# In the second block's plain attention stages, transposes are issued ahead of the next unit's scores

## What is computed

```python
def hybrid_layer(x, mem, norm_g, w_in, w_out, mem_norm_g, w_mem_kv, qk_g):
    h = rms_norm(x, norm_g)
    proj = jnp.einsum('btd,de->bte', h, w_in)
    ...
    qa = rope(rms_norm(to_heads(a_q, N_HEADS_MOBA), qk_g[0]))
    ka = rope(rms_norm(to_heads(a_k, N_HEADS_MOBA), qk_g[1]))
    oa = from_heads(moba_attention(qa, ka, to_heads(a_v, N_HEADS_MOBA)))
    ...
    ob = from_heads(dilated_attention(qb, kb, to_heads(b_v, N_HEADS_DIL)))
    ...
    om = from_heads(memory_attention(qm, km, to_heads(m_v, N_HEADS_MEM)))
    y = jnp.concatenate([oa * jax.nn.silu(a_g), ob * jax.nn.silu(b_g), om * jax.nn.silu(m_g)], axis=-1)
    return x + jnp.einsum('btd,de->bte', y, w_out)
```

## Time and profile before

| | |
|---|---|
| median of three runs | 2457.07 us (2455.22 to 2459.62) |
| the profiled execution | 2454.57 us, its span 2452.7 us |
| TensorE busy | 2417.9 us, 99% of the span |
| VectorE busy | 1192.6 us, 49% |
| ScalarE busy | 985.3 us, 40% |
| GpSimd busy | 1126.6 us, 46% |
| granted TensorE clock, mean | 0.998 of full |

### The profile page before, as it was taken

How to read it: one execution, slowest core, us unless ns; L and a number is a source line. 1 busy time by engine, 2 the same in 40 slices (tenths; PEclk the granted TensorE clock), 3 DMA queues, 4 the chain that set the end, 5 groups by cost and what they waited for, 6 DMA issues and landing times.

```text
span 2452.7 us, 29903 instructions
## 1 busy us (share of the span) xinstructions
PE 2417.9 (99%) x10934; PEld 1917.5 (78%) x10934; DVE 1192.6 (49%) x1821; ACT 985.3 (40%) x1529; POOL 1126.6 (46%) x828
## 2 busy tenths in 40 slices
PE   9999999999999999999999999999999999999998
PEld 7888888668888888888888768888888676776766
DVE  6444106664555105555106664555126766557553
ACT  5333124553222214222124553222216678456773
POOL 5454455335555445455455335555445332452324
PEclk9999999999999999999999999999999999999999
DMA  4222223212222222222223212222333222222222
GB/s 177 103 86 103 103 86 119 86 57 100 101 103 86 103 101 89 103 87 102 103 86 119 86 58 99 100 103 86 103 135 108 69 84 69 73 104 82 87 68 87
DMA packets 37961, 233.18 MB, mean 95 GB/s; under 512 B 5232, under 2 KB 5360, under 8 KB 11376
## 3 DMA queue, kind: packets, MB, share of 16 engines
q1 hardware_dynamic: 36432, 226.51, 26.8%
q10 hardware_dynamic: 1440, 5.45, 0.6%
HBM read 223.55 MB, written 2.10 MB: 92 GB/s over the span
## 4 chain that ended last, share of the span: by engine, by line
issue 56%; POOL 42%; POOLq 1%; DMA 1%; ACT 0%; SPq 0%; ACTq 0%
POOL w_lo L471 42%; POOLq L481 0%; DMA x_sb<-in_x 0%; POOLq L485 0%; DMA raw<-in_stream 0%; ACT h_hi L1064 0%; ACT w_hi L1021 0%; SPq L434 0%; POOLq L231 0%; ACT sq L1060 0%; ACTq L1442 0%; SPq L435 0%; ACTq L1098 0%; ACT w_hi L1077 0%; ACT hraw L1060 0%
## 5 line engine op out<-in xcount | busy, mean ns | idle before, releaser
L471 POOL TENSOR_TENSOR w_lo<-raw,w_hi 128x512 fp32r<-128x512 f32 x824 | 1126.4, 1398 | 1325.5 <-ACT w_hi L1021 1314.9
L493 PE MATMUL ps<-h_hi,w_hi 128*128 128x512 f32 x2304 | 916.5, 398 | 4.8 <-DVE h_lo L1505 3.9
L495 PE MATMUL ps<-h_hi,w_lo 128*128 128x512 f32 x2304 | 898.5, 390 | 0.0
L494 PE MATMUL ps<-h_lo,w_hi 128*128 128x512 f32 x2304 | 897.8, 390 | 0.0
L1021 ACT ACTIVATE w_hi<-raw 128x1024 fp32r<-128x1024 f32 x410 | 411.6, 1052 | 1163.9 <-PE ps L495 1160.6
L493 PEld LDWEIGHTS ps<-h_hi,w_hi 128*128 128x128 f32 x2304 | 433.2, 188 | 102.2 <-issue 7.5
L495 PEld LDWEIGHTS ps<-h_hi,w_lo 128*128 128x128 f32 x2304 | 432.9, 188 | 92.0
L494 PEld LDWEIGHTS ps<-h_lo,w_hi 128*128 128x128 f32 x2304 | 433.3, 188 | 90.8 <-issue 4.1
L493 PE MATMUL ps<-hid_hi,w_hi 128*128 128x512 f32 x704 | 273.9, 389 | 0.0
L494 PE MATMUL ps<-hid_lo,w_hi 128*128 128x512 f32 x704 | 273.9, 389 | 0.0
L495 PE MATMUL ps<-hid_hi,w_lo 128*128 128x512 f32 x704 | 273.9, 389 | 0.0
(11 more groups left out here) (255 smaller groups left out, 2028.6 us busy)
## 6 DMA issues: line engine op xcount, KB each, us to landing
raw<-in_stream SPq DMA_DIRECT2D x205, 1024.0 KB, 4.8
hraw<-xs SPq DMA_DIRECT2D x96, 64.0 KB, 2.0
x_sb<-in_x SPq DMA_DIRECT2D x4, 512.0 KB, 7.5
out_x<-x_sb SPq DMA_DIRECT2D x8, 256.0 KB, 6.5
raw<-in_stream SPq DMA_DIRECT2D x4, 256.0 KB, 6.8
mem_sb<-in_mem ACTq DMA_DIRECT2D x1, 1024.0 KB, 4.9
rec_sb<-in_recip ACTq DMA_DIRECT2D x2, 512.0 KB, 4.7
memn<-in_mem ACTq DMA_DIRECT2D x1, 1024.0 KB, 5.4
```

The costliest lines, as they stand in the source:

```text
L471: gp.tensor_tensor(w_lo[:, s, c], raw[:, s, c], w_hi[:, s, c].bitcast(F32), ALU.subtract).then_inc(lo_split, 1)
L493: pe.matmul(dst, l_hi, r_hi, start=first, stop=False)
L494: pe.matmul(dst, l_hi, r_lo, start=False, stop=False)
L495: return pe.matmul(dst, l_lo, r_hi, start=False, stop=last)
```

## The change

`attention_step` of TensorE is cut into three parts with unchanged bodies: `begin` (scores of unit `s`), `finish` (outputs) and `turn` (transposes of the unit in front). Before, the order is always begin, finish, turn. After, it is turn, begin, finish in every step but step 0 of the plain stages, and the old one everywhere else. The diff, with the bodies left out:

```diff
             def attention_step(here, before, s, produce):
-                unit = lagged(here, before, s, 0)
-                if unit:
...
-                    scores(stage, u).then_inc(t_scores, 1)
-                unit = lagged(here, before, s, LAG_OUT)
...
-                unit = lagged(here, before, s, LAG_TR)
...
+                def begin():
+                    unit = lagged(here, before, s, 0)
...
+                        scores(stage, u).then_inc(t_scores, 1)
+
+                def finish():
+                    unit = lagged(here, before, s, LAG_OUT)
...
+                        outputs(stage, u).then_inc(t_o, 1)
+
+                def turn():
+                    unit = lagged(here, before, s, LAG_TR)
...
+                        mm.then_inc(t_tr, 1)
+
+                if here and not here.memory and not here.fast and s:
+                    turn()
+                    begin()
+                    finish()
+                else:
+                    begin()
+                    finish()
+                    turn()
```

More of the change, by code:

```diff
@@ L843, in attention_step @@
[L843 to L859, removed]
+                def begin():
+                    unit = lagged(here, before, s, 0)
+                    if unit:
+                        stage, u = unit
+                        if s == 0 and not here.memory:
+                            pe.wait_ge(hn_out, GROUPS * here.l + here.gi + 1)
+                        if u and stage.memory:
+                            pe.wait_ge(t_exp, stage.u0 + u)
+                        elif not stage.memory:
+                            pe.wait_ge(t_exp if u == 0 and before.memory else t_max, stage.u0 + u)
+                        scores(stage, u).then_inc(t_scores, 1)
@@ new lines, in finish @@
+                def finish():
+                    unit = lagged(here, before, s, LAG_OUT)
+                    if unit and ends_group(unit[1]):
+                        stage, u = unit
+                        pe.wait_ge(t_thi, stage.u0 + u + 1)
+                        if not stage.memory:
+                            pe.wait_ge(v_thi, 7 * stage.l + stage.gi)
+                        elif u >= TB:
+                            pe.wait_ge(t_y, stage.outs0 + 1)
+                        outputs(stage, u).then_inc(t_o, 1)
@@ new lines, in turn @@
+                def turn():
+                    unit = lagged(here, before, s, LAG_TR)
+                    if unit:
+                        stage, u = unit
+                        pe.wait_ge(t_att, stage.u0 + u + 1)
+                        if not stage.memory:
+                            pe.wait_ge(t_thi, stage.u0 + u)
+                        elif u >= 2:
+                            pe.wait_ge(t_thi, stage.u0 + u - 1)
+                        for h in range(2):
+                            for kb in range(stage.widths[u] // P):
+                                if stage.memory:
+                                    n = 256 * h + P * kb
+                                    dst, src = ps[:, 2 + u % 2, n:n + P], att2[:, h, 256 * (u % 2) + P * kb:256 * (u % 2) + P * kb + P]
+                                else:
+                                    att = weights(u) if stage.fast else att2
+                                    dst, src = ps[:, 2 + h, P * kb:P * kb + P], att[:, h, P * kb:P * kb + P]
+                                mm = pe.transpose(dst, src, const(C_ID))
+                        mm.then_inc(t_tr, 1)
```

## The result

The changed kernel takes 2473.01 us (median of five runs, 2468.30 to 2474.83); the kernel before took 2455.33 in the same comparison (2452.93 to 2459.62). The ratio is 1.007, with a 95% interval of 1.0059 to 1.0081. The forecast was 2470, in a range of 2464 to 2477. The profiled execution of the changed kernel took 2473.01 us with a span of 2471.1, 18.4 more than that of before.

A forecast was written before the change was run, and what follows sets the result against it. TensorE was taken to bound the kernel. 8 x 1.85 = 14.8, + 0.3, - 1.9 gave +13.2 us on the profiled 2454.57, so 2467.8; 2.5 more for the median gave 2470.3, range 2464 to 2477.

The forecast's parts named there:

- What bounds the kernel: Whole kernel: TensorE, busy for 99% of the span, so the change is worth what it does to its idle time.
- Step 2: Plain stages, eight times: two transposes go ahead of the scores and nothing waits; +0.09 us, by the low end -0.08.
- Step 4: Plain stages, eight times: four transposes ahead of the scores, which start 0.52 us later; next piece +0.10 us.
- The change of kind: TensorE going from transposes to scores: 0.20 us from last transpose to first score, 0.02 to 0.03 as low end.
- Step 6: Plain stages, eight times: transposes wait about 1.9 us for ACT's scaling, scores queue behind; next piece +1.76 us.
- A whole stage: Each of the eight plain stages: 0.09 + 1.76 = 1.85 us longer.
- Stage 2: Its step 2, twice: memory stage's outputs are passed too, ACT's scaling ends 0.1 us late; about 0.15 us more each.
- Given back: Fast stage 6, behind stage 5, twice: TensorE's wait of 1.1 us (line 899) shrinks by 0.97; -1.9 us.
- Rival C: Step 4's exponentials follow ACT's copy, so weights come as before; +6.5 us, 2463.5; chance 0.13.
- Rival D: Plain stages: DVE and ACT's chain paces them, TensorE's delay eats its own waits, not slower; 2460.5; chance 0.04.
- The forecast's own case: Whole kernel: waits grow and the clock holds or falls once; between 2466 and 2472.5, likeliest 2470; chance 0.50.
- rival B: Plain stages: two to five of eight new waits bring a clock fall; +3.4 to +8.5 us, 2473.7 to 2478.8; chance 0.30.

The follow-up runs named there:

- The two experiments with one part each: The turned order in step 6 alone, and in steps 2 and 4 alone, each against the kernel before: 2461.79 us and 2460.00 us against 2455.12.
- The stages-2-to-4 experiment: The turned order in stages 2 to 4 of both layers, stage 5 as before, against the kernel before: 2467.53 us against 2455.51, ratio 1.0051.
- the last two kernels above: New and old order, both with ACT's scaling ahead of two head-norm passes and DVE's reciprocal ahead of the head norm: 2454.02 and 2450.24 us against 2454.68.

## Why the forecast came out as it did

**What bounds the kernel.** Right. Only TensorE's idle time and clock explain the difference.

**Step 2.** Forecast +0.09, measured +0.02 at the place and +0.07 with the piece behind it. **Step 4.** Forecast +0.10, measured +0.02 and +0.05. The change of kind from transposes to scores was right, about 0.2 us; the transition into the transposes was priced slightly too high. In step 4 they start 0.11 behind the last value transpose, not 0.14, and follow each other 0.11 apart, not 0.13. This also makes the scores 0.43 late instead of 0.52.

**Step 6.** Forecast +1.76, with step 4's 0.10 in it, and a wait of 1.9 us, 15 in all. Measured +1.63 and +0.02, a wait of 1.87, 15.0 in all. That the wait came out so close is in part luck. The forecast had TensorE free at 1994.23, but by the earlier trace rows the last matmul ends at 1993.74 + 0.39 = 1994.13, so its own terms give 2.00; weights that were late by 0.43 and not 0.52 took most of this back. The two experiments with one part each split it as the forecast had it: 11.8 us of waits from the order in step 6 alone, and from the late scores of step 4 alone twice the wait of before.

**A whole stage.** Forecast 1.85, measured 1.78 to 1.81. **Stage 2.** Forecast 0.15 more, measured 0.14 more.

**Given back.** Forecast -1.9, measured -2.0, at the place named. The wait for `sq_lo` fell from 1.1 to 0.4 rather than 0.1. DVE's row that waits for the DMA stands there at

```profile
2079.85 0.69 DVE L1905 TENSOR_TENSOR xs<-xs,rope_sb 128x512 f32<-128x512 f32 x1 [2.21 <-DMA hraw<-xs]
```

with 2.21 us of idle time instead of 2.70. The stages-2-to-4 experiment shows that nothing is given back unless the delay comes directly ahead of stage 6.

**Rival C.** Wrong, as it was held to be unlikely. The exponentials are 0.79 us idle behind the copy, and steps 2 and 4 alone made the kernel slower. **Rival D** likewise: no waits but those of stage 6 were eaten.

**The clock, the term that was too small.** The forecast's own case, 2470, had the clock holding or falling once. In the profile it fell three times in plain stages, which is rival B (two to five), though at 1.55 us each and not 1.7; where the 0.15 stay wasn't traced. Without those falls the profiled execution would be at 2473.0 - 4.7 = 2468.3, and without the 1.1 us of the first block at 2467.2; the sum had given 2467.8. So the mechanism and its terms were right within 1 us, and it is the clock that carries the profiled execution above them.

That the median of 2473.0 lies only 3 above the forecast of 2470 is in part luck too. As a difference, the change cost 17.7 us where the sum had 13.2, 4.5 less. The forecast then added 2.5, the distance of the median of three runs from the profiled one; in the comparison with the changed kernel the kernel before has 2455.33, only 0.8 above that execution. This offset hid a part of the missing clock term. The result lies between the forecast's own case (2466 to 2472.5) and B (2473.7 to 2478.8). The step that failed is the reading of a wait of 1.8 us in front of line 493 "followed by no fall" as a sign that 1.9 us would be harmless: it put the clock at nothing, and three falls cost 4.7 us. One execution could not show this. The same wait, in the first block, whose program is the same in both kernels, stands in TensorE's timeline of before and of after as

```profile
535.23 0.50 PE L493 MATMUL ps<-h_hi,w_hi 128*128 128x512 f32 x1 [1.83 <-DVE h_lo L1505]
```

```profile
534.75 0.65 PE L493 MATMUL ps<-h_hi,w_hi 128*128 128x512 f32 x1 [1.82 <-DVE h_lo L1519]
```

and the second is followed by the fall at 534.94, the first by none. Over the twelve profiled executions this wait was followed by a fall in eight; the one that the forecast was read from was among the other four.

## What to carry to other kernels

Work that the bottleneck engine does ahead of an instruction that waits is cover for this wait. Before moving it behind, read from the trace when the producer ends: if it ends after the engine would arrive, all that stands behind the instruction is exposed, and an earlier turn for a consumer that has slack buys nothing. Where such a wait exists, shorten the producer's chain instead (here two passes and a table load of ACT, put behind the scaling), and look in the same trace at who is queued behind the moved work on every engine, or the wait only appears one step later.

## What the runs showed of the hardware

A wait of TensorE of 1.8 us or more was often followed by a fall of the granted clock to 1.2 GHz, and a wait of 1.5 us never: 0 of 28 at 1.45 to 1.55 us, 8 of 12 at 1.8, 7 of 16 at 1.87, 14 of 25 at 2.7, 6 of 8 at 3.0. Between 1.8 and 3.0 us no steady rise can be read from so few. Most falls lasted 3.41 us; three lasted 6.83, one behind a wait of 2.7 us and two behind waits of 3.0. In stage 3, one fall of 3.41 us cost 1.55. A single profile in which a wait brings no fall says little about the next execution. The Trainium skill (TensorE: Matmul & The Clock Gate, Why this matters for your kernels) advises against idle gaps of over about 3 us between bursts of matmuls. The runs here agree that gaps matter, but falls came behind waits of 1.8 us already, so in this kernel that advice is too generous by more than a microsecond.

The order of kinds on TensorE costs little. Transposes in f32 ahead of the f32 scores, in place of behind them, made stages 3 to 5 longer by 0.14 to 0.21 us each, for three such places in a stage, where nothing waited for ACT's weights (the last two kernels above).
